# Feed-forward weight tiles multiplied as seven products of quarters instead of eight, with GpSimd forming the weight sums

## What is computed

```python
def ffn(h, wg, wu, wd):
    return (jax.nn.silu(h @ wg) * (h @ wu)) @ wd
...
x = x + ga2 * ffn(modulate(rms_norm_2(x, norm_ffn[i]), sh2, sc2),
                  w_gate[i], w_up[i], w_down[i])
...
return rms_norm_2(x, norm_final)
```

## Time and profile before

| | us |
|---|---|
| median of 3 runs | 3799.99 (3798.98 to 3800.39) |
| the profiled execution | 3798.29 |
| its span, first to last instruction | 3796.5 |
| PE busy | 3391.9 (89%) |
| DVE busy | 1329.4 (35%) |
| ACT busy | 523.3 (14%) |
| POOL busy | 184.3 (5%) |
| DMA, mean | 153 GB/s |

### The profile page before, as it was taken

How to read it: one execution, slowest core, us unless ns; L and a number is a source line. 1 busy time by engine, 2 the same in 40 slices (tenths; PEclk the granted TensorE clock), 3 DMA queues, 4 the chain that set the end, 5 groups by cost and what they waited for, 6 DMA issues and landing times.

```text
span 3796.5 us, 57854 instructions
## 1 busy us (share of the span) xinstructions
PE 3391.9 (89%) x26734; PEld 2834.4 (75%) x26734; DVE 1329.4 (35%) x2027; ACT 523.3 (14%) x913; POOL 184.3 (5%) x249
## 2 busy tenths in 40 slices
PE   1799589999988999599997788888889999999997
PEld 1689478888876888444586677777778888888886
DVE  7543555215346521222443566665330000000001
ACT  1211001111210020300001433433110000000000
POOL 1100000000000000100000112111000000000000
PEclk6899689999998999799998899999999999999999
DMA  9732567635234534333575000000463444443442
GB/s 389 295 123 89 222 245 303 249 133 213 100 130 184 216 132 151 113 127 139 193 290 203 8 7 8 9 7 4 174 260 133 155 155 155 148 146 137 152 152 83
DMA packets 51812, 582.15 MB, mean 153 GB/s; under 512 B 7010, under 2 KB 7328, under 8 KB 8464
## 3 DMA queue, kind: packets, MB, share of 16 engines
q1 hardware_dynamic: 33664, 465.06, 32.5%
q0 software_dynamic: 17936, 113.85, 7.9%
HBM read 576.78 MB, written 2.10 MB: 152 GB/s over the span
## 4 chain that ended last, share of the span: by engine, by line
PE 79%; DVE 9%; DMA 7%; ACT 3%; issue 2%; POOL 0%; DVEq 0%; ACTq 0%; POOLq 0%
PE PS L1280 29%; PE PS L334 14%; PE PS L1359 8%; PE PS L575 6%; PE PS L331 4%; DMA ring<-in_w_vec_dram 3%; PE PS L1475 2%; PE PS L1478 2%; PE PS L1464 2%; PE PS L348 1%; DVE ring L193 1%; DMA ring<-in_w_start_dram 1%; DMA ring<-in_w_second_dram 1%; DVE ring L780 1%; ACT W L1690 1%
## 5 line engine op out<-in xcount | busy, mean ns | idle before, releaser
L1280 PE MATMUL PS<-H,ring 128*128 128x256 f32 (+2 forms) x4736 | 1156.1, 407 | 42.9 <-ACT H L1621 30.9
L1280 PEld LDWEIGHTS PS<-H,ring 128*128 128x128 f32 (+1 forms) x4736 | 902.5, 191 | 296.4 <-issue 151.5
L334 PE MATMUL PS<-H,ring 128*128 128x256 f32 x3072 | 698.2, 387 | 73.2 <-DMA ring<-in_w_first_dram 69.2
L334 PEld LDWEIGHTS PS<-H,ring 128*128 128x128 f32 x3072 | 589.7, 194 | 163.2 <-DMA ring<-in_w_first_dram 69.7
L1359 PE MATMUL PS<-Pj,ring 128*128 128x256 f32 x1408 | 304.2, 379 | 1.2 <-DVE small L1928 1.2
L1359 PEld LDWEIGHTS PS<-Pj,ring 128*128 128x128 f32 x1408 | 267.4, 190 | 37.9 <-issue 1.6
L780 DVE SCALAR_TENSOR_TENSOR ring<-ring,H 128x2048 f32<-128x2048 f32 x96 | 219.1, 2289 | 161.6 <-DMA ring<-in_w_vec_dram 153.5
L575 PE MATMUL PS<-H,ring 128*128 128x256 f32 x1024 | 222.5, 379 | 2.9 <-DVE H L1031 2.9
L1922 DVE TENSOR_TENSOR Pj<-W,PS 128x512 f32 (+1 forms) x22 | 15.1, 687 | 597.3 <-PE PS L1280 597.3
L575 PEld LDWEIGHTS PS<-H,ring 128*128 128x128 f32 x1024 | 194.4, 190 | 30.0 <-issue 3.6
L331 PE MATMUL PS<-ring,H 128*128 128x256 f32 x768 | 172.0, 387 | 0.0
(11 more groups left out here) (401 smaller groups left out, 3112.4 us busy)
## 6 DMA issues: line engine op xcount, KB each, us to landing
ring<-in_w_second_dram SPq DMA_DIRECT2D x105, 2048.0 KB, 7.8
ring<-in_w_first_dram SPq DMA_DIRECT2D x76, 2048.0 KB, 8.0
ring<-in_w_vec_dram POOLq DMA_DIRECT2D x96, 1024.0 KB, 6.7
ring<-in_w_second_dram SPq DMA_DIRECT2D x32, 1408.0 KB, 6.0
ring<-in_w_start_dram SPq DMA_DIRECT2D x16, 2048.0 KB, 10.1
Pj<-in_x_dram SPq DMA_DIRECT2D x1, 2048.0 KB, 10.6
H<-in_cvecs_dram POOLq DMA_DIRECT2D x2, 1024.0 KB, 13.8
H<-in_cvecs_dram POOLq DMA_DIRECT2D x1, 2048.0 KB, 10.0
```

What stands on the lines that cost most here:

```text
L334: mm = pe.matmul(PS[:, t % 2, half * T:(half + 1) * T], ring[:, t % 2, k, half * P:(half + 1) * P], hT[:, k, :], start=(k == 0), stop=(k = ...
L1280: mm = pe.matmul(PS[0:cols, bank(q, half), 0:width], ring[:, q % RING].rearrange("p k n -> p (k n)")[:, k * 2 * cols + half * cols:k * 2 * ...
```

## The change

The products of gate, up and down are made by Strassen's scheme in Winograd's form. A tile's weight (up to 2048 rows x 256 columns) is cut into four quarters (upper and lower half of its chunks, left and right 128 columns), the activations into four as well (upper and lower half of the chunks, first and last 128 tokens). Instead of eight products of quarters there are seven, each of 8 (or 6) matmuls with 128 columns.

- Host: tiles of the feed-forward part are laid out quarter by quarter (`quartered`). The down weights come as 24 tiles (8 pairs of output chunks x 3 tiles of 16, 16 and 12 chunks) instead of 32.
- POOL: for each of the 68 tiles four elementwise sums over 128 x 1024 (128 x 768 for the short tiles), one of them in place in the ring, three into one of two side buffers in `W`. It waits for the tile's load, for the tile two before it to be multiplied, and twice for its own last sum.
- PE: `seven`, 56 (or 42) matmuls with 128 columns; the first three products need no weight sum, the last four wait for one each. No hardware loops.
- DVE: `right_sums` makes the four activation sums, once for `mix` ahead of the first tile (PE waits for it, `ff_t`), and once for each third of the hidden activations (`down_t`; the first during the gate and up tiles, the others behind the last of them). `outputs` puts the seven results together with four additions per tile (per three tiles in down), after which the Silu and the product are over SBUF operands.
- ACT: copies region 0 of each result out of PSUM, and takes Silu of the finished gate result.

```diff
-NDN = 2 * KC
+NDN = 3 * NOUT
...
-        tiles += [("w_down_2", h * DFF // 2, P * j, FC // 2, P) for h in range(2)]
+    for j in range(NOUT):
+        tiles += [("w_down_2", KC * P * g, TW * j, k_of(g), TW) for g in range(3)]
...
+    def quarter(q, n, nk=KC):
+        a = nk // 2 * P
+        return ring[:, q % RING].rearrange("p k n -> p (k n)")[:, n * a:(n + 1) * a]
...
+    def right(t, j, s):
+        a = t.shape[1] // 2
+        return t[:, a * j:a * j + a, s * P:s * P + P]
...
+        sums = S("ff_sum")
+        pool.wait_ge(S("h_ready_2").sem, S("h_ready_2").start + 3)
+        for n in range(2 * NFF + NDN):
...
+            pool.wait_ge(load[q % RING].sem, loaded(q))
+            if n > 1:
+                pool.wait_ge(tiles_done.sem, multiplied(q - 2))
...
+            sums.inc(pool.tensor_tensor(s_[:, 0], quarter(q, 2, nk), quarter(q, 3, nk), ALU.add))
+            pool.wait_ge(sums.sem, sums.start + 4 * n + 1)
+            sums.inc(pool.tensor_tensor(quarter(q, 2, nk), quarter(q, 0, nk), quarter(q, 2, nk), ALU.subtract))
+            sums.inc(pool.tensor_tensor(s_[:, 1], s_[:, 0], quarter(q, 0, nk), ALU.subtract))
+            pool.wait_ge(sums.sem, sums.start + 4 * n + 3)
+            sums.inc(pool.tensor_tensor(s_[:, 2], quarter(q, 1, nk), s_[:, 1], ALU.subtract))
...
+        def seven(q, n, x, t, bank2, nk=KC, first=True, last=True):
...
+            side, h = S_[n % 2], nk // 2
+            plan = ((0, quarter(q, 0, nk), right(x, 0, 0), 0), (1, quarter(q, 1, nk), right(x, 1, 0), 0), (2, quarter(q, 3, nk), t[:, 3], 0),
+                    (5, side[:, 0], t[:, 0], 1), (6, quarter(q, 2, nk), t[:, 2], 2), (3, side[:, 1], t[:, 1], 3), (4, side[:, 2], right(x, 1, 1), 4))
+            for r, w, m, after in plan:
+                if after:
+                    need_sum(4 * n + after)
+                for k in range(h):
+                    mm = pe.matmul(regions(bank2, r), w[:, k * P:(k + 1) * P], m[:, k, :], start=(first and k == 0 and r in (0, 5)), stop=(last and k == h - 1),
+                                   skip_group_check=True)
+            mm.then_inc(tiles_done.sem, 1)
+        need(S("ff_t"), 1)
+        for n in range(2 * NFF):
+            q = Q_FF + n
             ready(q)
-            product(q, lambda k: mix[:, k, :], T)
...
+            seven(q, n, mix, T_ff, n % 2)
...
+                if j == 0:
+                    need(S("down_t"), g + 1)
+                seven(q, 2 * NFF + 3 * j + g, hid(g), T_dn[g], j % 2, k_of(g), g == 0, g == 2)
...
+            do(f(u_[n % 2], regions(n % 2, 0), ACT.Copy), S("ff_first"))
...
+        def right_sums(x, t, done):
...
+            a, b, c, d = right(x, 0, 0), right(x, 0, 1), right(x, 1, 0), right(x, 1, 1)
+            do(v.tensor_tensor(t[:, 0], b, a, ALU.subtract))
+            settle()
+            do(v.tensor_tensor(t[:, 1], d, t[:, 0], ALU.subtract))
+            do(v.tensor_tensor(t[:, 2], d, b, ALU.subtract))
+            settle()
+            do(v.tensor_tensor(t[:, 3], t[:, 1], c, ALU.subtract), done)
...
+        def outputs(c, n, first):
...
+            settle()
+            need(S("ff_first"), first)
+            do(v.tensor_tensor(c[:, 0:5:4, :], u_[n].unsqueeze(1).to_broadcast([P, 2, P]), regions(n, 1, 4, 2), ALU.add))
+            settle()
+            do(v.tensor_tensor(c[:, 5:7, :], c[:, 4, :].unsqueeze(1).to_broadcast([P, 2, P]), regions(n, 5, 7), ALU.add))
+            settle()
+            do(v.tensor_tensor(c[:, 1:4:2, :], c[:, 5:7, :], regions(n, 4, 6), ALU.add))
+            return v.tensor_tensor(c[:, 2, :], c[:, 6, :], regions(n, 2), ALU.subtract)
...
+            if n % 2:
+                need(S("ff_silu"), n // 2 + 1)
+                v.wait_ge(evac[1].sem, read(Q_FF + n) + 1)
+                do(v.tensor_tensor(Pj[:, n - 1:n + 1, :], flat(cg)[:, 0:2 * T].rearrange("p (a t) -> p a t", a=2), flat(cu)[:, 0:2 * T].rearrange("p (a t) -> p a t", a=2), ALU.mult))
+            if n == 19:
+                settle()
+                right_sums(hid(0), T_dn[0], S("down_t"))
+        settle()
+        right_sums(hid(1), T_dn[1], S("down_t"))
+        for j in range(NOUT):
+            if j == 0:
+                right_sums(hid(2), T_dn[2], S("down_t"))
```

More of the change, by code:

```diff
@@ L162, in inc @@
     def inc(self, ins, by=1, times=1):
-        self.turns = max(self.turns, Sig.layers)
+        if not self.name.endswith("_start"):
+            self.turns = max(self.turns, Sig.layers)
         self.n += by * times
@@ L1338, in pe_program @@
         need(S("h_ready_2"), 3)
-        with pe.Fori(0, 2 * NFF // 6) as it:
-            for q in range(Q_FF, Q_FF + 6):
-                ready(q, it)
-                product(q, lambda k: mix[:, k, :], T)
-        for q in range(Q_DN - 2, Q_DN):
-            ready(q)
[L1346 to L1365, removed]
+        need_sum = lambda n: need(S("ff_sum"), n)
+        def seven(q, n, x, t, bank2, nk=KC, first=True, last=True):
[9 more added lines that the diff above has]
+            mm.then_inc(tiles_done.sem, 1)
@@ L1663, in act_program @@
             do(f(mix[:, k, :], Pj[:, 44 + k, :], ACT.Identity, bias=mod2[:, 48 + k, 0:1]), S("h_ready_2") if k == KC - 1 else None)
[L1666 to L1676, removed]
+        for n in range(2 * NFF):
+            q = Q_FF + n
+            act.wait_ge(tiles_done.sem, multiplied(q))
+            do(f(u_[n % 2], regions(n % 2, 0), ACT.Copy), S("ff_first"))
+            if n % 2 == 0:
+                act.wait_ge(evac[0].sem, read(q) + 1)
+                do(f(cg[:, 0:4, :], cg[:, 0:4, :], ACT.Silu), S("ff_silu"))
+        for j in range(NOUT):
+            act.wait_ge(tiles_done.sem, multiplied(Q_DN + 3 * j + 2))
+            do(f(u_[j % 2], regions(j % 2, 0), ACT.Copy), S("ff_first"))
         need(S("x_last"), 1)
@@ L1923, in dve_program @@
[L1923 to L1937, removed]
@@ L1938, in dve_program @@
-        with v.Fori(0, 5) as it:
-            for i in range(3):
-                down(i, it).then_inc(S("down_read").sem, 1)
-        do(down(15), S("x_last"))
+        def right_sums(x, t, done):
[6 more added lines that the diff above has]
+            do(v.tensor_tensor(t[:, 3], t[:, 1], c, ALU.subtract), done)
@@ new lines, in dve_program @@
+        need(S("h_ready_2"), 3)
+        right_sums(mix, T_ff, S("ff_t"))
+        for n in range(2 * NFF):
+            v.wait_ge(tiles_done.sem, multiplied(Q_FF + n))
+            outputs((cg, cu)[n % 2], n % 2, n + 1).then_inc(evac[n % 2].sem, 1)
+            if n % 2:
[5 more added lines that the diff above has]
+                right_sums(hid(0), T_dn[0], S("down_t"))
@@ new lines, in dve_program @@
+        settle()
+        right_sums(hid(1), T_dn[1], S("down_t"))
+        for j in range(NOUT):
+            if j == 0:
+                right_sums(hid(2), T_dn[2], S("down_t"))
+            v.wait_ge(tiles_done.sem, multiplied(Q_DN + 3 * j + 2))
+            do(outputs(cg, j % 2, 2 * NFF + j + 1), S("down_read"))
+            settle()
+            for half in range(2):
+                k = 2 * j + half
+                do(stt(xT[:, k, :], flat(cg)[:, half * T:half * T + T], mod2[:, 80 + k, 0:1], xT[:, k, :], ALU.mult, ALU.add),
+                   S("x_last") if k == KC - 1 else None)
@@ L2348, in tiled, with quartered @@
     return out
+def quartered(tiles):
+    out = np.zeros((len(tiles), P, KC * TW), np.float32)
+    for t, (w, r0, c0, nk, wide) in enumerate(tiles):
+        part = w[r0:r0 + nk * P, c0:c0 + wide].reshape(2, nk // 2, P, 2, P)
+        out[t, :, 0:nk * wide].reshape(P, 2, 2, nk // 2, P)[:] = part.transpose(2, 3, 0, 1, 4)
+    return out
 def turned(tiles):
@@ L2383 @@
             given["w_second"][q] = turned([(given[name][0], c0)])[0]
+        elif q >= Q_FF:
+            given["w_second"][q] = quartered([(given[name][0], r0, c0, *rest)])[0]
     c, c2, c_ctx = (given[n].reshape(D) for n in ("c", "c_2", "c_ctx_2"))
```

34 lines of the change are left out of this document (24 added, 10 removed).

## The result

| | before | after |
|---|---|---|
| median | 3800.19 us (3798.98 to 3802.14, 4 runs) | 3735.92 us (3731.82 to 3739.25, 4 runs) |
| the profiled execution | 3798.3 | 3731.8 |
| its span | 3796.5 | 3730.0 |
| PE matmul records | 26734 | 29902 |
| POOL busy | 184 us | 822 us |

The ratio of the times is 0.983, with a 95% interval of 0.9813 to 0.9847, so the kernel is 1.7% faster. In a second series it was 0.9834 (0.9821 to 0.9848), with 3736.09 us. The forecast was 3733 us, and faster.

The account below looks back on a forecast made before the run. PE's matmul stream was taken as the bound: 12.7 + 549.7 + 2.7 + 274.9 + 5.1 + 1.7 + 3.2 = 850.0 us against 916.9, so 3733 us. The range for 8 in 10 was 3707 to 3768.

Parts of the forecast that it names:

- ACT's last chunk to PE: Start: PE waits for the activation sums of `mix`, made in turns with POOL; 12.7 us, where 0.33 was.
- gate and up, with 2.7 for the clock: Gate and up tiles: 2464 matmuls x 0.2231 = 549.7 us, plus 2.7 us lost at the lower clock.
- wait at the second down tile: Passing to down: PE waits 5.1 us for DVE's activation sums of the second third, delayed by turns with POOL.
- clock behind it: After the wait at the second down tile: a lower granted clock costs PE 1.7 us.
- tail: End of down: ACT's copy, DVE's additions, products with addition and handovers after PE's last work, 3.2 us.
- the piece: From ACT's last chunk of the modulated input to the last addition into `xT`: 850.0 us, where 916.9 were.
- The stream: PE in gate, up and down: 0.2231 us per 128-column matmul, 824.6 us together where 915.0 were.
- rival 5: PE throughout: weight loads bind at 190 ns a record, 1404 us of matmuls, time 4310; chance 0.02.
- The lock: Start and passing to down: DVE instructions with two SBUF operands go in turns with POOL, giving 12.4 and 5.1 us.
- The hidden parts: Gate, up and down tiles: instruction fetch, weight sums and DVE's other work lie behind PE, put at 0.
- Rivals 3 and 4: POOL's sums bind every tile: from 2.9 us a sum (chance 0.10), slower than before from 3.13 (chance 0.08).
- rival 4: POOL bounds every tile, slower than before: at 3.3 us a sum, 14.2 a tile and 3845 us; chance 0.08.

Follow-up runs that it names:

- the split kernel: The kernel before, with each feed-forward matmul as two of 128 columns, all eight products and no sums: 3838.78 us, ratio 1.0089.

## Why the forecast was right, step by step

| step | forecast | measured |
|---|---|---|
| ACT's last chunk to PE | 12.7 | 11.2 |
| gate and up, with 2.7 for the clock | 552.4 | 552.9, with 2.5 |
| down, PE at work | 274.9 | 275.3 |
| wait at the second down tile | 5.1 | 3.3 |
| clock behind it | 1.7 | 1.4 |
| tail | 3.2 | 2.9 |
| the piece | 850.0 | 847.0 |

- The stream. 0.2231 us from 16 matmuls in the first block held for 3696: 0.2234. The weight loads were no bound at 190 ns a record. Their busy share is 100% now, where it was 88%, and PE was without gaps in both. That the share could be multiplied by 7/4, to 154%, was a step of my own, and it is what fails in rival 5: the records overlap, so their share cannot be added up.
- POOL. I took 2.54 us for a sum, twice a mask. Sums follow each other at 2.31 us, and a wait for the own last sum adds 0.1 and not 0.3. A tile's sums take 9.5 us and not 10.8. This is the term that was mis-sized, and with it the turns: POOL's turn is 2.2 us, 0.34 less than the 2.54, and DVE's sums at the start take 1.1 to 1.2. Three turns make 1.0 us of the 1.5 that the start is short; 0.3 are DVE's four sums and 0.2 the step to PE (0.1 us, not 0.3). In the middle a round of both takes 3.3 us where I had 3.7, and DVE's last sum comes 15.7 us behind the last up tile and not 17.6: that is the wait of 3.3 us in place of 5.1.
- The lock. That DVE and POOL go in turns came out of three instructions in the pair stage, and made 12 us here. Without it I would have said 3719. It is shown by the kernel in which only POOL's start was moved. One reading under it was weak: the 0.69 us that I took for an undisturbed DVE instruction is L1922, which has an operand in PSUM. The product of the same size with both operands in SBUF takes 0.69 too, with POOL quiet, so the reading holds.
- The hidden parts. DVE's additions and the turns that made them longer, ACT's copies, the sums for the down tiles made during the gate and up tiles, and the instruction fetch (3.85 MB where it was 3.01) cost PE nothing: it has no gap in 552.9 us.
- The total. The piece gave 69.9 us where 66.9 were forecast, and in the medians 64.3. The 3 us that the piece was better than forecast and the some 4 us lost ahead of it nearly cancel. That part of the agreement is luck.
- Rivals 3 and 4 had their mechanism right, POOL as the bound of every tile, and it sets in only with more sums. With four sums of 2.31 us POOL is far from it. With five it needs 11.9 or 12.3 us a tile, and they cost next to nothing. With six it takes 14.24 on average, and the kernel is slower than before: 3845 us, which is what rival 4 had worked out for 14.2 us a tile.

The balance of the change follows from the split kernel. With matmuls of 128 columns in both, seven products in place of eight are worth 946.7 - 829.6 = 117.1 us (PE at work in the two windows of either). The finer matmuls cost 31.8, start, wait and tail 16.5 more than before, and 1.1 us of gap between up and down goes: 69.9.

## What to carry to other kernels

One of eight products saved is worth 12.5% of PE's stream only if the pieces cost what the whole did. Price the smaller matmul by a run of it in the trace, start to start: here the finer matmuls took 31.8 us of the 117.1 that the eighth product was worth. Before giving GpSimd work that runs beside VectorE, list VectorE's instructions with two SBUF operands that someone waits for, which took 3.3 us here in place of 1.2. Hold GpSimd back there, or give VectorE the work if it has the time. And the reserve of a helper engine (here GpSimd beside TensorE) is a threshold: one sum more a tile cost nothing that could be told, a second one 108 us.

## What the runs showed of the hardware that I had not expected

- GpSimd's elementwise sum of two 128 x 1024 float32 operands takes 2.31 us start to start in a row, VectorE's 1.14 to 1.26. A mask over 512 columns took 1.27, so doubling the size costs a factor of 1.8.
- The same wait of 3.3 us was followed by a granted clock of 0.83 over 8.5 us in one kernel and of 0.62 over 8.1 us in another. So the same short wait cost 1.4 or 3.1 us through the clock. What decides between them no run shows. The start of the feed-forward part differs in the same way within one kernel: 0.63 and 0.82 over the first 8 us in two profiles of the kernel before.
- LDWEIGHTS records of 192 ns covered 552 us without a gap while a load was begun every 112 ns: they overlap, and a busy share of 100% did not slow the stream.
